# RMS norm statistics with tokens on partitions, in a two-block transformer kernel on one core

## The chip, the cores and the metric

The kernel runs on one core of one Trainium2 chip. The metric is the device time of the core in microseconds, the median of several runs; lower is better. The profile is of one separate execution.

## The reference

One sequence goes through a first block (gated linear attention layer, then an S5 layer, each with attention over a memory of 256 tokens) and a second block (an RWKV and pooling layer with an MLP, then a differential attention layer with an MLP). All of it is float32, width 1024, 512 tokens; the second block puts 16 meta tokens ahead, which makes 528. What the change touches is the norm:

```python
def rms_norm(x, w):
    xf = x.astype(jnp.float32)
    y = xf * lax.rsqrt(jnp.mean(xf * xf, axis=-1, keepdims=True) + EPS)
    return (y * w.astype(jnp.float32)).astype(x.dtype)

mem_n = rms_norm(mem, mem_norm_w)                 # 256 tokens
for i in range(DEPTH):                            # first block
    h = rms_norm(x, norm_w[i])
    ...
    x = x + y @ w_out[i]
x = rms_norm(x, final_norm_w)
for i in range(DEPTH):                            # second block
    hn = rmsnorm(h, g[0]); m = mixer(hn)
    h = h + rmsnorm(m, g[1])
    f = sq_relu_mlp(rmsnorm(h, g[2]))
    h = h + rmsnorm(f, g[3])
```

## The kernel before

All activations lie with features on the 128 partitions and tokens along the free axis: a tensor of width 1024 is eight tiles k of 128 features by 512 or 528 tokens. With 528 tokens a PSUM bank (512 float32 columns) doesn't hold a row of them, so such work goes in two halves of 264 (`HALVES`, line 45). Weights come in units of 128x1024 through a ring of four buffers, loaded by the sync engine. Most matrix products (class `Gemm`, line 101) split both operands into a rounded high part and a low rest and add three products (lines 256, 259, 261). ScalarE makes the high part of each weight unit (`make_high`, line 358), GpSimd the low part (`make_low`, line 349), and TensorE waits for the low part before it begins a unit.

Each engine has its own program. The kernel is a list of stages, and each engine goes through that list in the same order, doing its part of each stage; between engines there are only counting semaphores (`squared`, `summed`, `rooted`, `inverted`, `normed` and others for the norms). The numbers a stage waits for are worked out when the kernel is built, from `b.norms`, a table of how far each semaphore has counted.

A norm is the stage `Rms` (line 462). The squares of the tiles are written by ScalarE. For norms with `added=True` the squares are made while the matrix product ahead of the norm stores its tiles, and VectorE adds them up (`add`, line 521) but for the last, so that TensorE has only two groups of products left (lines 558 and 562). For the others TensorE takes the squares of each k as they come (line 568), ScalarE being at most two squares ahead. These products multiply a 128x128 matrix of ones by the squares, so that every partition of the result has the sum over features, for each token. ScalarE then takes the root of sum / width + eps (line 543), VectorE the reciprocal of the whole 128 by tokens tile (line 580) into `b.inv`, and then scales tile after tile (line 588). Depending on the norm VectorE also adds the result onto x (`onto`, line 585) or subtracts the high part from it (`hi`, `lo`, lines 549 and 593). When the norm feeds a product, ScalarE makes the first high part of its weights directly behind the root (line 546), before the high parts of the tiles.

In the list there are nine such norms and, inside the gated linear attention, four more over 512 features per head. The nine: the memory's (256 tokens) and the first layer's (512 tokens), one behind the other at the start and followed on VectorE by the S5 tables (line 1083) and on TensorE by the memory's key product (line 266 in the profile); the S5 layer's, ahead of the product u; the final norm of the first block; ahead of the second block's first product (528 tokens, not added); behind ev_out and behind the first MLP (528 tokens); behind od_out and behind the last MLP (512 tokens). Behind three of the last four stands a `LateRms` (line 605), a norm whose statistic is worked out while its product already runs on unscaled values; it stays as it is. Its `scalar` starts with the high part of weight unit 1, and it waits for the x tiles that the norm before it finishes. `TokenInverse` (line 685) turns the reciprocals of one late norm into columns with products that move a single column (line 696).

The profile's line numbers are those of the code printed here.

Of the kernel before, what the change touches and what calls it, by code (L numbers as in the profile page):

```python
# [17 lines left out]
ACT = mybir.ActivationFunctionType  # L18
# [5 lines left out]
P = 128  # L24
D = 1024
KD = D // P
# [435 lines left out]
class Rms(Stage):  # L462
# [2 lines left out]


    def __init__(self, b, x, n, ranges, width, eps, w, out, banks, needs, stay=(), view=None, onto=None,
                 hi=None, lo=None, each=None, added=False):
        self.each = each
        self.added = added  # L470
        self.b, self.x, self.n, self.ranges, self.width = b, x, n, ranges, width
        self.eps, self.w, self.out, self.banks, self.needs, self.stay = eps, w, out, banks, needs, stay
        self.view = view or (lambda ap: ap)
        self.onto = onto
        self.at = dict(b.norms)
        self.tokens = sum(w for _, w in ranges)
        b.norms["squared"] += n
        b.norms["summed"] += 1 if added else n
        b.norms["added"] += n - 2 if added else 0
        b.norms["rooted"] += len(ranges)  # L480
        b.norms["inverted"] += 1
        b.norms["ready"] += n
        self.rooted = (b.rooted, b.norms["rooted"])
        self.ready = (b.normed, b.norms["ready"])
        self.tile = lambda k: (b.normed, self.at["ready"] + k + 1)
        if onto:
            self.tile = lambda k: (b.summed_onto, self.at["summed_onto"] + k + 1)
            b.norms["summed_onto"] += n
            self.ready = (b.summed_onto, b.norms["summed_onto"])
        self.feeds = None  # L490
        self.hi, self.lo = hi, lo
        if hi:
            b.norms["parts"] += n
            self.ready = (b.out_lo, b.norms["parts"])
# [34 lines left out]
    def scalar(self, act):  # L529
        b, at = self.b, self.at  # L530
# [8 lines left out]
        act.wait_ge(b.summed, at["summed"] + (1 if self.added else self.n))  # L539
        if at["inverted"]:  # L540
            act.wait_ge(b.inverted, at["inverted"])
        for bank, (t0, tn) in zip(self.banks, self.ranges):
            b.nc.scalar.activation(b.root[:, t0:t0 + tn], b.ps[:, bank, 0:tn], ACT.Sqrt,
                                   bias=b.eps[self.eps], scale=1.0 / self.width).then_inc(b.rooted, 1)
        if self.feeds:
# [5 lines left out]
    def tensor(self, pe):  # L551
        b, at = self.b, self.at
        for s, v in self.stay:
            pe.wait_ge(s, v)
        if self.added:
            pe.wait_ge(b.added, at["added"] + self.n - 2)
            for bank, (t0, tn) in zip(self.banks, self.ranges):
                b.nc.tensor.matmul(b.ps[:, bank, 0:tn], b.ones[:, :], b.sq[:, 0, t0:t0 + tn], start=True, stop=False)
            pe.wait_ge(b.squared, at["squared"] + self.n)
            last = self.slot(self.n - 1)  # L560
            for bank, (t0, tn) in zip(self.banks, self.ranges):
                ins = b.nc.tensor.matmul(b.ps[:, bank, 0:tn], b.ones[:, :], b.sq[:, last, t0:t0 + tn], start=False, stop=True)
            ins.then_inc(b.summed, 1)
            return
        for k in range(self.n):
            pe.wait_ge(b.squared, at["squared"] + k + 1)
            for bank, (t0, tn) in zip(self.banks, self.ranges):
                ins = b.nc.tensor.matmul(b.ps[:, bank, 0:tn], b.ones[:, :], b.sq[:, k % 2, t0:t0 + tn],  # L568
                                         start=(k == 0), stop=(k == self.n - 1))
            ins.then_inc(b.summed, 1)  # L570

    def vector(self, dve):
        b, at = self.b, self.at
        if self.added:
            for k in range(self.rest, self.n - 1):
                self.add(dve, k)
        dve.wait_ge(*self.rooted)
        if at["ready"]:
            dve.wait_ge(b.normed, at["ready"])
        b.nc.vector.reciprocal(b.inv[:, 0:self.tokens], b.root[:, 0:self.tokens]).then_inc(b.inverted, 1)  # L580
        dve.wait_ge(b.inverted, at["inverted"] + 1)
        for k in range(self.n + 2):
            if self.onto and 1 <= k <= self.n:
# [222 lines left out]
class Gla(Stage):  # L806
# [6 lines left out]
    def __init__(self, b, m, z, needs):  # L813
# [22 lines left out]
        for h in range(GLA_HEADS):  # L836
            o = m.o[h]
            last = min(4 * h + 5, self.steps)
            self.rms.append(Rms(b, lambda k, o=o: o[:, k, :], DV // P, FULL, DV, EPS,
                                lambda k: b.col("gla_out_norm_w", k), lambda k, o=o: o[:, k, :], [0],  # L840
                                [(self.saved, 4 * h + 4)], [(self.masked, last), (self.token_keys, last)]))
# [1902 lines left out]
def build(nc, a, out):  # L2744

    with ExitStack() as ctx:
        b = Board(nc, ctx)
# [9 lines left out]
        tables = constants()  # L2757
# [109 lines left out]
        def mix_tile(s):  # L2867
            if s < KD:
# [17 lines left out]
        rms = Rms(b, lambda k: mem[:, k, :], KD, MEMS, D, EPS, lambda k: b.col("mem_norm_w", k),  # L2886
                  lambda k: b.memn[:, k, :], [0], [loads_in], [loads_in])
# [38 lines left out]
        tables = S5Tables(b, t5, a, [rms.ready, (b.summed, 2 * KD)])  # L2926
# [530 lines left out]
```

## Time and profile before

| | us |
|---|---|
| median of 3 runs | 3248.36 |
| lowest, highest run | 3247.49, 3256.5 |
| the profiled execution's own time | 3260.21 |
| its span, first to last instruction | 3257.9 |
| TensorE products busy | 2957.2 (91%) |
| TensorE weight loads busy | 2403.1 (74%) |
| VectorE busy | 1383.3 (42%) |
| GpSimd busy | 1070.2 (33%) |
| ScalarE busy | 970.0 (30%) |

The profile calls the engines PE (products), PEld (weight loads), DVE, ACT, POOL and SP. Products are pipelined, so PE's busy time is not PE at its peak. The chain of waits follows the work that ended last back from the end, step by step. PEclk is the clock granted to TensorE as a share of 2.4 GHz; its mean over the span is 0.959. A float32 product appears as two passes, each with a weight load (LDWEIGHTS) and a MATMUL. Its shape is given as result type, so 128x264 means 264 moving columns.

### The profile page before, as it was taken

Reading aid. Unit: us, or ns where it says so; the run is one execution under the profiler, and the core shown is the slowest. Engines: PE = TensorE matmul, PEld = TensorE weight load, DVE = VectorE, ACT = ScalarE, POOL = GpSimd, SP = SyncE. Lnnn points to the kernel's source line nnn. Section 1 sums busy time; section 2 is a strip of 40 time slices with the busy share of each in tenths; the row PEclk is TensorE's granted clock in tenths of the full one; section 3 lists DMA queues with packets and bytes.
Section 4 is the critical chain, followed back from the end, with each engine's and each line's share of the span. In section 5 each row is a group of like instructions: output and inputs, shape, how many; then the busy total and the mean of one; then the engine's idle time right before and its main releaser. Section 6 shows DMA issues by size and latency. Waiting matters only on the chain.

```text
span 3257.9 us, 45682 instructions
## 1 busy us (share of the span) xinstructions
PE 2957.2 (91%) x18278; PEld 2403.1 (74%) x18278; DVE 1383.3 (42%) x2233; ACT 970.0 (30%) x1551; POOL 1070.2 (33%) x743
## 2 busy tenths in 40 slices
PE   6887899899899899998978887899998989989997
PEld 4666467677788488786767775799996857768886
DVE  5787264510217511202158453470724055374352
ACT  2222254222212246323244332312123115431221
POOL 0332022444324078444422200144443330234442
PEclk9998899999999899999999996999999989999999
DMA  4897011244562279222221000222222200122222
GB/s 141 262 278 247 7 52 44 68 145 152 172 190 95 78 195 245 92 96 78 92 69 59 22 3 20 65 91 89 89 89 79 84 26 1 39 71 97 97 91 78
DMA packets 130704, 324.96 MB, mean 100 GB/s; under 512 B 54096, under 2 KB 54736, under 8 KB 129760
## 3 DMA queue, kind: packets, MB, share of 16 engines
q1 hardware_dynamic: 95904, 221.29, 21.2%
q0 software_dynamic: 30272, 88.88, 9.7%
q10 hardware_dynamic: 4352, 12.25, 1.0%
q8 instruction: 133, 2.18, 0.3%
q14 instruction: 43, 0.35, 0.0%
HBM read 288.38 MB, written 33.95 MB: 99 GB/s over the span
## 4 chain that ended last, share of the span: by engine, by line
PE 71%; DVE 17%; DMA 4%; issue 3%; POOL 2%; ACT 2%; DVEq 0%; ACTq 0%; SPq 0%; POOLq 0%
PE ps L256 17%; PE ps L259 16%; PE ps L261 16%; PE ps L266 3%; DMA d_pb<-arena 3%; PE ps L2473 2%; DVE h L588 1%; PE ps L738 1%; PE ps L568 1%; POOL ring_r L349 1%; PE ps L748 1%; PE ps L2484 1%; DVE inv L580 1%; PE ps L1591 1%; PE ps L1332 1%
## 5 line engine op out<-in xcount | busy, mean ns | idle before, releaser
L349 POOL TENSOR_TENSOR ring_r<-ring,high 128x1024 fp32r<-128x1024 f32 x327 | 819.6, 2506 | 1574.1 <-ACT high L358 1573.9
L256 PE MATMUL ps<-h_hi,high 128*128 128x512 f32 (+1 forms) x2112 | 733.4, 356 | 51.4 <-POOL ring_r L349 18.5
L261 PE MATMUL ps<-h_hi,ring_r 128*128 128x512 f32 (+1 forms) x2112 | 661.1, 348 | 0.0
L358 ACT ACTIVATE high<-ring 128x1024 fp32r<-128x1024 f32 x359 | 379.5, 1057 | 896.3 <-PE ps L256 769.5
L259 PE MATMUL ps<-h_r,high 128*128 128x512 f32 (+1 forms) x1920 | 643.9, 345 | 0.0
L256 PEld LDWEIGHTS ps<-h_hi,high 128*128 128x128 f32 x2112 | 400.7, 190 | 130.3 <-issue 59.3
L261 PEld LDWEIGHTS ps<-h_hi,ring_r 128*128 128x128 f32 x2112 | 370.2, 190 | 53.3
L259 PEld LDWEIGHTS ps<-h_r,high 128*128 128x128 f32 x1920 | 365.7, 190 | 41.8 <-issue 1.4
L259 PE MATMUL ps<-f_r,high 128*128 128x264 f32 (+1 forms) x832 | 261.2, 326 | 0.0
L256 PE MATMUL ps<-f_hi,high 128*128 128x264 f32 (+1 forms) x768 | 236.6, 321 | 0.0
L256 PE MATMUL ps<-z_hi,high 128*128 128x512 f32 x488 | 197.0, 404 | 16.5 <-POOL ring_r L349 10.7
L261 PE MATMUL ps<-f_hi,ring_r 128*128 128x264 f32 (+1 forms) x768 | 205.0, 321 | 0.0
L261 PE MATMUL ps<-z_hi,ring_r 128*128 128x512 f32 x488 | 192.5, 394 | 0.0
L259 PEld LDWEIGHTS ps<-f_r,high 128*128 128x128 f32 x832 | 156.8, 188 | 14.4
L2831 ACT ACTIVATE arena<-ps 128x512 f32<-128x512 f32 (+4 forms) x102 | 58.2, 574 | 331.7 <-PE ps L261 242.4
L256 PEld LDWEIGHTS ps<-f_hi,high 128*128 128x128 f32 x768 | 144.4, 188 | 11.4
L259 PE MATMUL ps<-z_lo,high 128*128 128x512 f32 x360 | 145.3, 404 | 0.0
L261 PEld LDWEIGHTS ps<-f_hi,ring_r 128*128 128x128 f32 x768 | 127.0, 188 | 11.0
L3264 DVE CAST f_hi<-f x64 | 128.9, 2014 | 8.5 <-DVE f L3262 1.2
L256 PEld LDWEIGHTS ps<-z_hi,high 128*128 128x128 f32 x488 | 92.9, 190 | 44.7 <-issue 14.2
L259 PE MATMUL ps<-z_hi,high 128*128 128x512 f32 x280 | 112.2, 401 | 0.0
L261 PEld LDWEIGHTS ps<-z_hi,ring_r 128*128 128x128 f32 x488 | 93.4, 191 | 22.4
(433 smaller groups left out, 4419.7 us busy)
## 6 DMA issues: line engine op xcount, KB each, us to landing
ring<-in_units SPq DMA_DIRECT2D x402, 512.0 KB, 3.3
d_ca<-arena POOLq DMA_DIRECT2D x16, 640.0 KB, 9.5
arena<-d_ca POOLq DMA_DIRECT2D x16, 640.0 KB, 7.2
arena<-d_q POOLq DMA_DIRECT2D x32, 256.0 KB, 8.2
d_pb<-arena POOLq DMA_DIRECT2D x16, 512.0 KB, 11.1
arena<-d_pb POOLq DMA_DIRECT2D x16, 512.0 KB, 4.1
arena<-d_ca POOLq DMA_DIRECT2D x16, 512.0 KB, 5.0
arena<-d_k POOLq DMA_DIRECT2D x128, 64.0 KB, 4.1
```

The lines of the kernel that those rows point to most:

```text
L256: part = mm(acc, hi[:, cols], self.x_hi(k)[:, t0:t0 + tn], start=(k == 0), stop=False)
L259: mm(acc, hi[:, cols], self.x(k)[:, t0:t0 + tn], start=False, stop=False)
L261: ins = mm(acc, w[:, cols], self.x_hi(k)[:, t0:t0 + tn], start=False, stop=(k == self.kt - 1))
L266: ins = mm(acc, w[:, k % 8 * P:(k % 8 + 1) * P], self.x(k)[:, t0:t0 + tn], start=(k == 0), stop=(k == self.kt - 1))
L349: eng.tensor_tensor(b.ring_r[:, slot, :], b.ring[:, slot, :], self.high[:, j % 2, :], ALU.subtract).then_inc(b.unit_lo, 1)
L358: b.nc.scalar.activation(self.high[:, j % 2, :], b.ring[:, u % RING, :], ACT.Copy).then_inc(b.unit_hi, 1)
L568: ins = b.nc.tensor.matmul(b.ps[:, bank, 0:tn], b.ones[:, :], b.sq[:, k % 2, t0:t0 + tn], start=(k == 0), stop=(k == self.n - 1))
L580: b.nc.vector.reciprocal(b.inv[:, 0:self.tokens], b.root[:, 0:self.tokens]).then_inc(b.inverted, 1)
L588: b.nc.vector.scalar_tensor_tensor(out=self.out(k), in0=self.view(self.x(k)), scalar=self.w(k), in1=self.view(b.inv[:, 0:self.tokens]), op ...
L2473: ins = mm(to, m.prob[:, j % 3, c, k0:k0 + kn], m.diag[:, j % 2, c, :], start=(c == 0), stop=(c == 1))
L2831: return nc.scalar.activation(to, ps, ACT.Copy, scale=1.0 if scale is None else scale)
L3264: nc.vector.tensor_copy(hi, t).then_inc(mlp_parts, 1)
```

## The change

`Rms` gets an argument `turned`, true for all but the four norms of the gated linear attention. A turned norm has the squares as stationary operand, 88 tokens at a time (528 = 6 x 88) or 128 (512 = 4 x 128, 256 = 2 x 128), and one column of ones as moving operand: the sum of each token then lies on its own partition, in one column per tile. Root and reciprocal are taken of this block of 88x6 (128x4, 128x2) numbers, both into the tile `b.root`. To have the reciprocals on every partition again, TensorE multiplies: the stationary operand is one column of reciprocals read with a step of zero as 128 columns, the moving one the identity, so each result column is one token's reciprocal on all partitions. ScalarE copies the result from PSUM into `b.inv`. The scalings are unchanged.

```diff
@@ Rms.__init__
-        b.norms["summed"] += 1 if added else n
+        b.norms["summed"] += (1 if added else n) + (1 if turned else 0)
-        b.norms["rooted"] += len(ranges)
+        b.norms["rooted"] += 2 if turned else len(ranges)
+        self.turned = turned
+        self.rows = 88 if self.tokens % P else P
+        self.tiles = [(o, slice(o * self.rows, (o + 1) * self.rows)) for o in range(self.tokens // self.rows)]
@@ Rms.scalar, behind the waits for the sums and the last reciprocal
+        if self.turned:
+            rows, many = self.rows, len(self.tiles)
+            b.nc.scalar.activation(b.root[0:rows, 0:many], b.ps[0:rows, self.banks[0], 0:many], ACT.Sqrt,
+                                   bias=b.eps[self.eps][0:rows], scale=1.0 / self.width).then_inc(b.rooted, 1)
+            act.wait_ge(b.summed, at["summed"] + (1 if self.added else self.n) + 1)
+            first, parts, wide = self.banks[0], len(self.ranges), self.ranges[0][1]
+            b.nc.scalar.activation(b.inv[:, 0:self.tokens].rearrange("p (r t) -> p r t", r=parts),
+                                   b.ps[:, first:first + parts, 0:wide], ACT.Copy).then_inc(b.rooted, 1)
-        for bank, (t0, tn) in zip(self.banks, self.ranges):
+        for bank, (t0, tn) in [] if self.turned else zip(self.banks, self.ranges):
@@ Rms.tensor, each place with products of ones; self.spread(pe) also behind the last of them
+            if self.turned:
+                ins = self.token_sums(pe, k % 2, k == 0, k == self.n - 1)
+    def token_sums(self, pe, slot, start, stop):
+        b = self.b
+        for o, tok in self.tiles:
+            ins = b.nc.tensor.matmul(b.ps[0:self.rows, self.banks[0], o:o + 1], b.sq[:, slot, tok], b.ones[:, 0:1],
+                                     start=start and o == 0, stop=stop and o == len(self.tiles) - 1)
+        return ins
+    def spread(self, pe):
+        if not self.turned:
+            return
+        b, rows = self.b, self.rows
+        pe.wait_ge(b.inverted, self.at["inverted"] + 1)
+        per = len(self.tiles) // len(self.ranges)
+        for o, _ in self.tiles:
+            at = o % per * rows
+            ins = b.nc.tensor.matmul(b.ps[:, self.banks[0] + o // per, at:at + rows],
+                                     b.root[0:rows, 8 + o:9 + o].broadcast_to([rows, P]), b.ident[0:rows, 0:rows],
+                                     start=True, stop=True)
+        ins.then_inc(b.summed, 1)
@@ Rms.vector
-        dve.wait_ge(*self.rooted)
-        b.nc.vector.reciprocal(b.inv[:, 0:self.tokens], b.root[:, 0:self.tokens]).then_inc(b.inverted, 1)
+        if self.turned:
+            rows, many = self.rows, len(self.tiles)
+            dve.wait_ge(b.rooted, at["rooted"] + 1)
+            b.nc.vector.reciprocal(b.root[0:rows, 8:8 + many], b.root[0:rows, 0:many]).then_inc(b.inverted, 1)
+            dve.wait_ge(*self.rooted)
+        else:
+            (as before)
```

## Rows read from the trace of the kernel before

**Rows 1.** The page's chain of waits, whole span: shares by engine, by line
```profile
PE 71%; DVE 17%; DMA 4%; issue 3%; POOL 2%; ACT 2%; DVEq 0%; ACTq 0%; SPq 0%; POOLq 0%
PE ps L256 17%; PE ps L259 16%; PE ps L261 16%; PE ps L266 3%; DMA d_pb<-arena 3%; PE ps L2473 2%; DVE h L588 1%; PE ps L738 1%; PE ps L568 1%; POOL ring_r L349 1%; PE ps L748 1%; PE ps L2484 1%; DVE inv L580 1%; PE ps L1591 1%; PE ps L1332 1%
```
**Rows 2.** Line 580: durations min/median/max in ns, first and last start, forms
```profile
L580 DVE RECIPROCAL inv<-root x13: 1752/3352/3453, 27.9 to 3240.9; 128x512 f32<-128x512 f32 x9, 128x528 f32<-128x528 f32 x3, 128x256 f32<-128x256 f32 x1
```
**Rows 3.** Chain in order of time, from 2072 us: start, length, what
```profile
2073.74 1.13 PE ps L558 x4
...
2075.79 0.86 ACT root L543 x2
...
2076.68 3.46 DVE inv L580
...
2080.16 0.78 DVE h L588
...
2080.97 0.71 DVE x L585
```
**Rows 4.** The same chain, from 3238 us
```profile
3238.02 0.14 issue
3238.16 1.10 PE ps L558 x2
...
3240.15 0.70 ACT root L543
...
3244.25 0.76 DVE h L588
```
**Rows 5.** Instructions of line 696 (as rows 2), then their stretch of the timeline
```profile
L696 PEld LDWEIGHTS ps<-c_ident,inv x10: 93/192/192, 2578.8 to 2579.8; 128*128 128x128 f32 x8, 128*16 128x16 f32 x2
...
2578.94 1.08 PE L696 MATMUL ps<-c_ident,inv 128*128 128x1 f32 x10
```
**Rows 6.** Small operations: count | busy us, mean ns | idle; last a timeline row
```profile
L2596 DVE RECIPROCAL arena<-arena 128x2 f32<-128x2 f32 x32 | 5.1, 160 | 0.3
L2512 ACT ACTIVATE arena<-ps,arena 128x16 f32<-128x16 f32 x16 | 4.3, 268 | 0.0
...
2073.03 0.60 ACT L2831 ACTIVATE h<-ps 128x528 f32<-128x528 f32 x1
```
**Rows 7.** Timeline of the first two norms: start, length, engine, line [idle before]
```profile
27.28 0.47 ACT L543 ACTIVATE root<-ps,c_eps 128x256 f32<-128x256 f32 x1
...
28.32 7.53 PE L568 MATMUL ps<-sq,c_ones 128*128 128x512 f32 x16 [1.60 <-ACT sq L538]
...
36.67 13.62 PE L266 MATMUL ps<-memn,ring 128*128 128x256 f32 x62 [0.82 <-issue]
...
54.52 15.77 PE L266 MATMUL ps<-memn,ring 128*128 128x256 f32 x64 [3.79 <-ACT arena L2831]
```
**Rows 8.** Timeline ahead of the product u
```profile
811.58 1.28 ACT L543 ACT_TABLE_LOAD   x1
...
814.59 2.33 POOL L349 TENSOR_TENSOR ring_r<-ring,high 128x1024 fp32r<-128x1024 f32 x1 [1.08 <-ACT high L358]
816.98 3.26 DVE L588 SCALAR_TENSOR_TENSOR h<-x,cols,inv 128x512 f32<-128x512 f32 x3
```
**Rows 9.** Timeline and chain of the second block's first norm
```profile
1647.80 10.32 PE L568 MATMUL ps<-sq,c_ones 128*128 128x264 f32 x32 [5.63 <-ACT sq L538]
...
1662.52 2.12 DVE h L588 x3
...
1671.72 1.05 ACT high L358
```
**Rows 10.** Stretches of 1 us: length, PE PEld DVE ACT POOL busy (x), PEclk, DMA
```profile
1642.00:1643.00 1.00, 0.17 (x1) 0.00 (x0) 0.07 (x1) 0.69 (x1) 1.00 (x3) 1.00 0.77 316
...
1646.00:1647.00 1.00, 0.00 (x0) 0.00 (x0) 0.96 (x3) 0.00 (x0) 0.00 (x0) 0.62 0.54 197
...
1652.00:1653.00 1.00, 1.00 (x4) 0.80 (x3) 0.00 (x0) 0.42 (x1) 0.00 (x0) 0.50 0.00 0
```

More of the change, by code:

```diff
@@ L467, in __init__ @@
     def __init__(self, b, x, n, ranges, width, eps, w, out, banks, needs, stay=(), view=None, onto=None,
-                 hi=None, lo=None, each=None, added=False):
+                 hi=None, lo=None, each=None, added=False, turned=True):
         self.each = each
@@ L556, in tensor @@
             pe.wait_ge(b.added, at["added"] + self.n - 2)
-            for bank, (t0, tn) in zip(self.banks, self.ranges):
+            if self.turned:
+                self.token_sums(pe, 0, True, False)
+            for bank, (t0, tn) in [] if self.turned else zip(self.banks, self.ranges):
                 b.nc.tensor.matmul(b.ps[:, bank, 0:tn], b.ones[:, :], b.sq[:, 0, t0:t0 + tn], start=True, stop=False)
@@ L560, in tensor @@
             last = self.slot(self.n - 1)
-            for bank, (t0, tn) in zip(self.banks, self.ranges):
+            if self.turned:
+                ins = self.token_sums(pe, last, False, True)
+            for bank, (t0, tn) in [] if self.turned else zip(self.banks, self.ranges):
                 ins = b.nc.tensor.matmul(b.ps[:, bank, 0:tn], b.ones[:, :], b.sq[:, last, t0:t0 + tn], start=False, stop=True)
             ins.then_inc(b.summed, 1)
+            self.spread(pe)
             return
@@ L566, in tensor @@
             pe.wait_ge(b.squared, at["squared"] + k + 1)
-            for bank, (t0, tn) in zip(self.banks, self.ranges):
+            if self.turned:
+                ins = self.token_sums(pe, k % 2, k == 0, k == self.n - 1)
+            for bank, (t0, tn) in [] if self.turned else zip(self.banks, self.ranges):
                 ins = b.nc.tensor.matmul(b.ps[:, bank, 0:tn], b.ones[:, :], b.sq[:, k % 2, t0:t0 + tn],
@@ L570, in tensor @@
             ins.then_inc(b.summed, 1)
+        self.spread(pe)
+    def token_sums(self, pe, slot, start, stop):
[16 more added lines that the diff above has]
+        ins.then_inc(b.summed, 1)
     def vector(self, dve):
@@ L576, in vector @@
                 self.add(dve, k)
-        dve.wait_ge(*self.rooted)
         if at["ready"]:
             dve.wait_ge(b.normed, at["ready"])
-        b.nc.vector.reciprocal(b.inv[:, 0:self.tokens], b.root[:, 0:self.tokens]).then_inc(b.inverted, 1)
+        if self.turned:
+            rows, many = self.rows, len(self.tiles)
[3 more added lines that the diff above has]
+        else:
+            dve.wait_ge(*self.rooted)
+            b.nc.vector.reciprocal(b.inv[:, 0:self.tokens], b.root[:, 0:self.tokens]).then_inc(b.inverted, 1)
         dve.wait_ge(b.inverted, at["inverted"] + 1)
@@ L840, in __init__ @@
                                 lambda k: b.col("gla_out_norm_w", k), lambda k, o=o: o[:, k, :], [0],
-                                [(self.saved, 4 * h + 4)], [(self.masked, last), (self.token_keys, last)]))
+                                [(self.saved, 4 * h + 4)], [(self.masked, last), (self.token_keys, last)], turned=False))
         self.done = (self.multiplied, z.body_outs * z.iters)
@@ L2925, in build @@
         t5.par = view(14336, 13, 192)
-        tables = S5Tables(b, t5, a, [rms.ready, (b.summed, 2 * KD)])
+        tables = S5Tables(b, t5, a, [rms.ready, (b.summed, 2 * KD + 2)])
         stages.append(tables)
```

## The prediction

> **What bounds the kernel now.** I read the chain of waits first. It stands on TensorE for 71% of the span and on VectorE for 17%, and the norms' scalings and reciprocals (lines 588 and 580) have 1% each in its rounded shares [rows 1]. The matmuls take most of the time, so what matters is where TensorE stands still. The lines view gives the reciprocal thirteen times at about 3.35 us [rows 2]. Nine of these belong to the norms that the change turns; four are the gated linear attention's, which keep the old way. The chain in order of time shows a norm behind a matmul stage: products with ones, root, reciprocal, first scaling, first sum, each released by the one before, with TensorE quiet from the sums to the next stage's first product [rows 3, 4]. These are stretches in which time saved reaches the end.
>
> **The price of the new pieces.** The nearest thing to the new products is line 696, five float32 products with one moving column. Each is two passes of weight load and product; ten passes start in 1.08 us, of which two load 16 columns, so a 128-column pass costs about 0.12 us and the last result needs 0.14 us more [rows 5]. The other pieces: a reciprocal of 128x2 takes 0.16 us, an activation of 128x16 from PSUM 0.27 us, a 128x528 copy out of PSUM 0.60 us [rows 6]. I put the small root at 0.25, the small reciprocal at 0.16, the copy at 0.60 (0.40 for 256 tokens, between the last two), and 0.04 per handover, as between root and reciprocal in [rows 3].
>
> **From root to first scaling.** Before, with 528 tokens: 2075.79 to 2080.16, 4.37 us [rows 3]. After, with six tiles of 88: 0.25 root + 0.04 + 0.16 reciprocal + 0.04 + spreading + 0.04 + 0.60 copy + 0.04. The spreading is six products, twelve passes, each loading 128 columns (one column of reciprocals broadcast): 12 x 0.12 + 0.14 = 1.58. Sum 2.75, saved 1.62. With 512 tokens before: 3240.15 to 3244.25, 4.10 us [rows 4]; after, with four tiles, eight passes: 0.96 + 0.14 = 1.10, sum 2.27, saved 1.83.
>
> **The sums.** With 512 tokens, four products of 512 columns (ones by the sum so far and by the last square, each in two passes) run from 3238.16 to the root at 3240.15, 1.99 us [rows 4]; sixteen new passes cost 16 x 0.12 + 0.14 = 2.06, a loss of 0.1. With 528 tokens, eight passes of 264 columns take 2073.74 to 2075.79, 2.05 us [rows 3]; the new twenty-four load 88 columns each. In [rows 5] a 16-column load takes 93 ns where a 128-column one takes 192, and interpolated that is 155 ns for 88, so I take 0.10 per pass: 2.4 + 0.14 = 2.54, a loss of 0.5. Bounds for a pass: 0.075 (the loads alone, scaled) to 0.12, so the sums gain 0.1 or lose 1.0.
>
> The Trainium skill, "TensorE: Matmul & The Clock Gate", section "Part 2: What happens when you issue a matmul", says the weight load's time goes with the columns loaded and not with the rows. By it an 88-column pass would be 88/128 of 0.12, an estimate of 0.083 us, and the sums of 528 tokens would take 2.1 us and lose 0.1 instead of 0.5; by the row of this trace the load shortens less than in proportion. The same rule gives the spreading nothing for its 88 rows, as I have counted.
>
> **Norm by norm.**
> - The memory's norm and the first norm (27 to 40 us). The squares of the second now stand behind the first's copy on ScalarE. Before, they stood behind the first root, which ends at 27.75 [rows 7]. Now: root from 27.28, 0.25 + 0.04 + 0.16 + 0.04 + two tiles spread (four passes, 0.62) + 0.04 + copy 0.40 = 28.83, so 1.1 us late. The eight sums were sixteen passes in 7.53 us, 0.94 each k; sixty-four new passes at 0.12 are 7.7, a loss of 0.2 to 0.5. Then the chain from the root saves 1.83. Net saved 0.3. Also, the memory's key product starts on the second norm's copy instead of its root, 1.4 late and 2.23 instead of 0.70 behind the root's start, so at 39.6 instead of 36.67; this is covered, since TensorE later waits 3.79 us for ScalarE to empty its banks, until 54.52 [rows 7]. Without the cover it would cost 2.9.
> - Norm ahead of the product u (813 us). The root follows a table load that ends at 812.86 behind other ScalarE work, so nothing in the sums matters; from the root on 1.83 saved. The high part of the next weights (line 358, 1.05 us) and its POOL half (2.33 us) used to hide under the reciprocal [rows 8]. They now start behind the copy: counted from the root's start, 2.23 + 1.05 + 0.05 + 2.33 = 5.7 us, while the first lower half h_r, behind three scalings, is there at 2.27 + 3 x 1.09 + 0.7 = 6.2. Still hidden, by 0.5.
> - Final norm of the first block (1642 us), 512 tokens: 1.83 - 0.1 = 1.7.
> - First norm of the second block (1648 to 1671 us), not added up on VectorE: eight steps of sums. Before, 10.32 us for thirty-two passes [rows 9], the first half of it at a granted clock of 0.50, 1.2 GHz [rows 10]. New: ninety-six passes. At full clock 9.6 + 0.14 = 9.7, a gain of 0.6; if the first 3.7 us stay at half clock, 11.4, a loss of 1.1. Before, the clock fell 4 us after TensorE's last product, with TensorE quiet in between; now the spreading stands in the middle of that quiet. I take 0. From the root 1.62 saved. The weights' high and low parts now end 2.7 + 1.05 + 2.33 = 6.1 us after the root's start, and the first lower half of h at 2.75 + 2.12 + 0.7 = 5.6, so TensorE begins 0.5 later than VectorE would allow; but the first tile goes by VectorE's pace, and the second starts only on the high part made at 1671.72 [rows 9], behind all of ScalarE's work on h, which moves with VectorE. So 1.6.
> - Norms behind ev_out and the first MLP (2076, 2469 us), 528 tokens: 1.62 - 0.5 = 1.1 each. The free high part of unit 1 behind the copy (1.06 us) stays under the first scaling and sum (1.5 us, [rows 3]).
> - Norms behind od_out and the last MLP (2866, 3241 us), 512 tokens: 1.7 each. The last one ends in the output's DMAs, which follow tile by tile.
>
> Sum: 0.3 + 1.8 + 1.7 + 1.6 + 1.1 + 1.1 + 1.7 + 1.7 = 11.0 us. VectorE also loses some 27 us of busy time, worth nothing beyond this. The profiled execution took 3260.21 us (span 3257.9); minus 11.0 it is 3249.2. The runs' median is 3248.36, 11.85 under the profiled one, so the forecast for the median is 3237.4 us.
>
> **Bounds.** The sum hangs on the pass, since there are 64 + 96 + 2 x 24 + 3 x 16 of them in sums on the path and 5 x 8 + 3 x 12 in spreadings. Below: 0.10 in the spreadings and 0.075 in the sums of 88 columns take 1.5 and 3.6 off, 16 us saved. Above: 0.13 for every pass adds 0.8 in the spreadings, 2.9 at 1648, 0.7 at 2076 and at 2469, 0.6 at 28 and 0.5 in the sums of 512 tokens, 5 us saved. Own range of the forecast: 3232 to 3243.
>
> **Rivals.**
> 1. *Half clock in the new products (slower).* The two long runs of sums, at 28 and 1646 us, become runs of one-column products, and the granted clock falls to 0.50 in them. For it: after TensorE's quiet the clock is at 0.50 for 6.8 us [rows 10], and in no row does a run of one-column products last longer than 1.1 us. Against: the weight loads keep TensorE occupied throughout, and line 696 ran at 1.00. Price: at half clock a pass doubles. Sixty-four at 0.24 are 15.4 instead of 7.5 us, ninety-six at 0.20 are 19.2 instead of 10.3: 16.8 us more. If the spreadings are caught as well, five cost 8 x 0.12 and three 12 x 0.12 more, 9 us in all. It decides from 11 us, that is when both runs are caught. Outcome: -11 + 17 to -11 + 26, +6 to +15, middle 3259 us. The Trainium skill, "TensorE: Matmul & The Clock Gate", section "Part 1: The HAM clock gate (the "warmup" mystery)", says that the clock is throttled by default and that activity releases it; by it this rival depends on whether such products count, which no row here settles.
> 2. *A narrow pass costs more than in line 696 (no change).* At 0.15 us a pass the spreadings lose 2.3, the sums at 1648 4.8, those at 2076 and 2469 2.4, those at 28 1.9 and those of 512 tokens 1.4: 12.8 us, which leaves +2, 3250 us. For it: nothing here loads a broadcast column as weights, or strings so many loads together, and VectorE's handover to TensorE took 0.14 us [rows 4] where I count 0.04. Against: the ten passes of [rows 5], back to back behind other work.
> 3. *The first savings are given back.* Those at 28 and 813 us feed stages in which DMAs also bound work; then only the second block's and the final norm's 8.9 us stay: 3239.5 us. Against: the chain at both places runs through VectorE. This lies in the forecast's own range and I count it there.
>
> **How the numbers follow.** What a measurement of this kernel can tell from no change is 0.3%, 9.7 us. Forecast (with rival 3) 60%, centre 3237.4, of which seven in ten pass 9.7 us. Rival 1 22%, two thirds of it beyond +9.7. Rival 2 18%, all within. Faster 0.60 x 0.72 = 0.43; slower 0.14; same 0.43. The range takes the forecast's own and rival 2, and the lower half of rival 1: 3231 to 3258.
>
> **What would show it.** The small reciprocal on 88 and 128 partitions at about 0.16 us nine times; copies of 0.6 us into inv; root to first scaling 2.75 and 2.27 us; the sums at 1648 near 10 us and at 28 near 8 us with the granted clock beside them. Wrong it would be if a pass costs over 0.15 us, if the clock is at 0.50 in either run of sums, or if the quiet behind a norm has not become shorter where root to scaling has.

## The result, and the profile after

The changed kernel takes 3268.82 us (median of 4 runs, 3262.95 to 3273.97) against 3250.56 us of the kernel before in the same session (4 runs, 3247.49 to 3256.5). The ratio is 1.0044, 95% interval 1.0023 to 1.0065: slower by 0.4%. The profiled execution has a span of 3268.1 us at a mean granted clock of 0.956; before it was 3257.9 us at 0.959. The forecast was 3237.4 us.

First the new pieces, each line's instructions with the shortest, median and longest duration in ns; they answer to [rows 2, 5, 6].

```profile
L623 DVE RECIPROCAL root<-root x9: 165/178/188, 28.1 to 3251.1; 128x4 f32<-128x4 f32 x5, 88x6 f32<-88x6 f32 x3, 128x2 f32<-128x2 f32 x1
...
L547 ACT ACTIVATE root<-ps,c_eps x9: 262/263/265, 27.7 to 3250.7; 128x4 f32<-128x4 f32 x5, 88x6 f32<-88x6 f32 x3, 128x2 f32<-128x2 f32 x1
...
L551 ACT ACTIVATE inv<-ps x9: 384/597/612, 29.6 to 3253.4; 128x512 f32<-128x512 f32 x5, 128x528 f32<-128x528 f32 x3, 128x256 f32<-128x256 f32 x1
```

Root, reciprocal and copy cost about what was forecast (0.25, 0.16, 0.60). What comes out wrong stands in three other places. The timeline of the first two norms (start, length, engine, line), to be read beside [rows 7]:

```profile
27.73 0.26 ACT L547 ACTIVATE root<-ps,c_eps 128x2 f32<-128x2 f32 x1
...
30.53 13.81 PE L595 MATMUL ps<-c_ones,sq 128*128 128x1 f32 x64 [0.99 <-ACT sq L541]
...
44.38 0.26 ACT L547 ACTIVATE root<-ps,c_eps 128x4 f32<-128x4 f32 x1 [2.79 <-PE ps L595]
...
47.78 4.61 PE L266 MATMUL ps<-memn,ring 128*128 128x256 f32 x10 [0.73 <-issue]
```

The sixty-four one-column passes take 13.81 us, 0.216 each, where 16 wide ones took 7.53. TensorE is never idle in these 13.81 us. The second norm's first scaling comes at 47.72 us instead of 39.99, and the memory's key product at 47.78 instead of 36.67.

What the clock was in this run has to be read from durations, because the column PEclk can't be relied on this early: in every profile it reads 1.00 from the start to its first fall, also where TensorE works at half pace. These are the clock's row (columns as below), the run's weight loads, those of the sixteen wide passes before, and the loads of the same form in the changed kernel's sums at 1644 us, where the durations agree with the 1.00 of the column (ns: shortest, median, longest):

```profile
30.53:44.34 13.81, 13.81 (x64) 13.72 (x64) 2.72 (x7) 4.24 (x7) 0.00 (x0) 1.00 0.01 1
L595 PEld LDWEIGHTS ps<-c_ones,sq x64: 287/333/333, 30.5 to 43.9; 128*128 128x128 f32 x64
L568 PEld LDWEIGHTS ps<-sq,c_ones x16: 186/189/190, 28.3 to 34.8; 128*128 128x128 f32 x16
L595 PEld LDWEIGHTS ps<-c_ones,sq x16: 186/192/192, 1643.6 to 1645.3; 128*128 128x128 f32 x16
```

A load of 128 columns that takes 192 ns at 1.00 takes 333 here, and 333 is also what it takes in the spreading at 1665 us, where PEclk reads 0.50. So the run went at half clock, by its durations and not by the column. In the kernel before, the loads take 333 ns only in the memory norm's first sums, from 20.4 to some 24 us, and then 190.

The second block's first norm, beside [rows 9], and then the granted clock around it (length, PE, PEld, DVE, ACT, POOL busy with counts, PEclk, DMA share, GB/s), beside [rows 10]:

```profile
1650.16 14.24 PE L595 MATMUL ps<-c_ones,sq 128*88 128x1 f32 x96 [2.15 <-ACT sq L541]
...
1665.05 2.86 PE L608 MATMUL ps<-c_ident,root 88*128 88x88 f32 x12 [0.64 <-DVE root L623]
...
1668.59 4.21 DVE L635 SCALAR_TENSOR_TENSOR h<-x,cols,inv 128x528 f32<-128x528 f32 x3 [3.60 <-ACT inv L551]
...
1669.59 2.65 POOL L349 TENSOR_TENSOR ring_r<-ring,high 128x1024 fp32r<-128x1024 f32 x1 [22.91 <-ACT high L358]
```

```profile
1645.00:1647.00 2.00, 1.37 (x10) 1.28 (x10) 0.18 (x1) 0.26 (x1) 1.68 (x4) 0.86 0.87 297
1647.00:1650.00 3.00, 1.01 (x5) 0.72 (x4) 1.32 (x2) 1.13 (x2) 0.00 (x0) 0.50 0.93 271
1650.00:1664.00 14.00, 13.84 (x95) 13.84 (x95) 4.07 (x7) 4.61 (x8) 0.00 (x0) 0.50 0.01 2
1664.00:1668.00 4.00, 3.27 (x15) 2.95 (x15) 0.19 (x1) 0.32 (x2) 0.00 (x0) 0.50 0.00 0
1668.00:1676.00 8.00, 2.43 (x11) 2.46 (x12) 7.41 (x9) 4.53 (x7) 2.65 (x1) 0.50 0.10 25
```

For 14 us TensorE is busy 13.84 us with products and with loads, and the clock stays at 0.50, 1.2 GHz. Before, it was back at full within the wide sums. These are the neighbouring stretches of the kernel before:

```profile
1647.00:1650.00 3.00, 2.20 (x5) 1.80 (x6) 3.00 (x6) 1.29 (x2) 0.00 (x0) 0.50 0.00 0
1650.00:1658.00 8.00, 8.00 (x28) 5.69 (x27) 1.70 (x3) 3.86 (x6) 0.00 (x0) 0.81 0.00 0
1658.00:1662.00 4.00, 0.12 (x1) 0.00 (x0) 2.96 (x1) 1.80 (x3) 1.97 (x1) 1.00 0.00 0
```

The three scalings in the norm's rows above take 4.21 us instead of the 2.12 of [rows 9], and GpSimd works beside them. The norm behind ev_out, timeline, beside [rows 3], has the same thing:

```profile
2082.32 2.76 PE L595 MATMUL ps<-c_ones,sq 128*88 128x1 f32 x24 [1.25 <-issue]
2085.12 0.26 ACT L547 ACTIVATE root<-ps,c_eps 88x6 f32<-88x6 f32 x1 [2.90 <-PE ps L595]
2085.48 0.19 DVE L623 RECIPROCAL root<-root 88x6 f32<-88x6 f32 x1 [10.14 <-ACT root L547]
2085.72 2.86 PE L608 MATMUL ps<-c_ident,root 88*128 88x88 f32 x12 [0.64 <-DVE root L623]
2088.62 0.61 ACT L551 ACTIVATE inv<-ps 128x528 f32<-128x528 f32 x1 [3.24 <-PE ps L608]
2089.12 1.05 ACT L358 ACTIVATE high<-ring 128x1024 fp32r<-128x1024 f32 x1
2089.26 0.77 DVE L635 SCALAR_TENSOR_TENSOR h<-h,cols,inv 128x528 f32<-128x528 f32 x1 [3.60 <-ACT inv L551]
2090.07 0.71 DVE L632 TENSOR_TENSOR x<-x,h 128x528 f32<-128x528 f32 x1
2090.25 2.73 POOL L349 TENSOR_TENSOR ring_r<-ring,high 128x1024 fp32r<-128x1024 f32 x1 [105.59 <-ACT high L358]
2090.69 2.85 DVE L635 SCALAR_TENSOR_TENSOR h<-h,cols,inv 128x528 f32<-128x528 f32 x1
```

Here the clock fell inside the sums, from 1.00 in the microsecond from 2082 to 0.50 in that from 2084, and they take 2.76 us; the experiments below show 2.01 for the same passes at 1.00. Two things more: the spreading takes 2.86 us, 0.24 a pass, so that root to first scaling is 4.14 us against 4.37 in [rows 3]; and the second scaling takes 2.85 us where one takes 0.77, because it meets GpSimd's low part. In the kernel before, the high part was made behind the root and the low part ran beside the reciprocal [rows 8]. Its company didn't lengthen the reciprocal: over 512 tokens it takes 3.35 us at 813.59 beside GpSimd, and 3.35 at 36.61 with GpSimd idle.

How far each place lies behind the kernel before, in us: first scaling of the second norm 7.7; start of the attention 8.6; first reciprocal of the gated linear attention 4.1; small reciprocal ahead of u 3.1; at 1645 us 3.0; at 1664 us 5.8; at 2085 us 8.8; at 2106 us 11.2; at 2480 us 11.0; at 2875 us 8.6; the end 10.2. In these two profiles the attention gives back 4.5 of the first loss, but over all profiles it doesn't. The first reciprocal of the gated linear attention starts at 475.0 to 484.1 us in the eight profiles whose first two norms are as before (482.1 in the kernel before), and at 485.6 to 493.1 in the four that have them turned with no product added, 9.3 later on average. The scatter of 8 to 9 us within each group is as large as the effects looked for: in 320 to 480 us the mean granted clock of the profiled executions lies between 0.86 and 0.94, with no order by kernel, and the kernel before alone ranged from 3242.3 to 3265.7 us over 33 runs. I rest the parts below on ratios and on the durations of instructions.

### The profile page after: what moved, and what is told of

Read it like the earlier page. It is cut to its first block, busy times and chain, and to the rows that moved or that the text cites. A ratio compares the mean times of both kernels' runs of the same rounds, so it can differ in the third digit from the quotient of the medians.

```text
span 3268.1 us, 46273 instructions
## 1 busy us (share of the span) xinstructions
PE 2983.3 (91%) x18566; PEld 2445.6 (75%) x18566; DVE 1365.9 (42%) x2233; ACT 971.6 (30%) x1557; POOL 1064.0 (33%) x743
## 4 chain that ended last, share of the span: by engine, by line
PE 71%; DVE 17%; DMA 4%; issue 3%; POOL 2%; ACT 2%; DVEq 0%; ACTq 0%; SPq 0%; POOLq 0%
PE ps L256 16%; PE ps L259 16%; PE ps L261 16%; PE ps L266 3%; DMA d_pb<-arena 2%; DVE h L635 2%; PE ps L2520 1%; PE ps L595 1%; PE ps L785 1%; PE ps L795 1%; PE ps L2531 1%; PE ps L1638 1%; PE ps L1379 1%; POOL ring_r L349 1%; PE ps L1469 1%
```

## The experiments

Each ratio is against the kernel before in the same session, with its 95% interval; the runs of one kernel are 6 to 12, those of the kernel before 25 to 33. They are told by question. "Turned" is a norm with the new statistics, "added" one whose squares VectorE sums first (six of the nine).

**Which norms lose?** Turned only where added, then only where not.

```diff
+        self.turned = turned = turned and added          # e2_added
+        self.turned = turned = turned and not added      # e4_long
```

> The changed kernel with only the six norms turned whose squares VectorE adds up (two groups of sums each); the memory's, the first layer's and the second block's first norm are as before the change. Theory A: the long runs of one-column products are gone, so are their 6.3 and 3.9 us and the spreadings at half clock there; 8 to 12 us less than the changed kernel, 3257 to 3261, still above the kernel before because of the POOL collisions at 813, 2090 and 2879 us. Rival (the loss is spread evenly over all nine norms): a third of it goes, near 3262.

> Only the three norms that VectorE doesn't add up are turned (the memory's and the first at 20 to 48 us, the second block's first at 1645 us); the six others are as before. Theory (the change's parts add up, and the long runs of sums at half clock are what makes it slower): the run at 28 us takes 13.8 instead of 7.5 us and that at 1645 us 14.2 instead of 10.3, the scaling behind the latter 4.2 instead of 2.1 us; 7 to 8 us lost at the first and 2 to 4 at the second, ratio 1.003 to 1.005, which times the 0.9997 of the six others alone gives the 1.0044 of the whole change. Rival (the loss at 28 us is given back behind it, where transfers and the half clock of the attention set the pace): ratio 1.000 to 1.001, and the whole change's 1.0044 has no owner.

Measured: 3251.1 us, ratio 0.9997 (0.9981 to 1.0012), for the six; 3264.31 us, 1.0035 (1.0018 to 1.0052), for the three. Their product is 1.0032, inside the interval of the whole. So the three norms that VectorE doesn't add up carry most of the loss, some 11 us, and the six bring no measurable gain. In the profile of the three, the runs of sums take what they took in the whole change: 13.81 us at 30.63 and 14.24 us at 1648.87.

**Is it the clock, and do wider products free it?** Once 64 columns of ones move in each sum instead of one, once a wide product of the old kind stands ahead of each k's sums.

```diff
-            ins = b.nc.tensor.matmul(b.ps[0:self.rows, self.banks[0], o:o + 1], b.sq[:, slot, tok], b.ones[:, 0:1],
+            ins = b.nc.tensor.matmul(b.ps[0:self.rows, self.banks[0], 64 * o:64 * o + 64], b.sq[:, slot, tok], b.ones[:, 0:64],
```
```diff
+                b.nc.tensor.matmul(b.ps[:, 6, 0:self.ranges[0][1]], b.ones[:, :],
+                                   b.sq[:, k % 2, 0:self.ranges[0][1]], start=True, stop=True)
                 ins = self.token_sums(pe, k % 2, k == 0, k == self.n - 1)
```

> The changed kernel with one edit: the sums move 64 columns of ones instead of one (the results stand 64 times side by side, the root reads every 64th column). Weight loads, their count and their order are the same. Theory A (the clock is at 0.50 in the two long runs of sums because of what is moved): the granted clock is at 1.00 again in most of both runs, the sums at 28 us take about 8 us instead of 13.8 and those at 1650 about 10 instead of 14.2, some 10 to 12 us less than the changed kernel, near 3258. Rival B (a narrow pass costs about 0.2 us by its weight load, whatever is moved): both runs as long as before or longer, time unchanged near 3268.

> The changed kernel, with one product of the old kind (ones by 256, 512 or 264 columns of squares, two passes) ahead of each k's one-column sums in the three norms that are not added up on VectorE; it adds work of no use. Theory (wide moving operands raise the granted clock, weight loads do not): the clock goes to 1.00 in both runs; one-column passes take 0.12 us at 128 columns and 0.083 us at 88; the run at 28 us is then 8 x (0.94 + 0.96) = 15.2 us and that at 1645 us 8 x (0.5 + 1.0) = 12 us, 2 less than the 14.2 us of the change in spite of the added work. Rival (the clock stays down for another reason, such as the one-column products pulling it down whatever stands between): passes stay at 0.21 and 0.147 us, the wide ones double, and the runs take 27 and 21 us.

Measured: 64 columns, 3263.0 us, 1.0025 (1.0009 to 1.0041); with the wide products 3292.49 us, 1.0115 (1.0093 to 1.0137). The row of the timeline of the first at the second block's first norm, then its clock (columns as above):

```profile
1643.33 14.34 PE L595 MATMUL ps<-c_ones,sq 128*88 128x64 f32 x96 [2.15 <-ACT sq L541]
```
```profile
1643.00:1658.00 15.00, 14.34 (x96) 14.16 (x96) 4.24 (x7) 5.04 (x9) 0.00 (x0) 0.50 0.01 2
```

The same two of the second:

```profile
1663.69 1.23 PE L584 MATMUL ps<-sq,c_ones 128*128 128x264 f32 x2
1664.71 1.83 PE L597 MATMUL ps<-c_ones,sq 128*88 128x1 f32 x12
```
```profile
1670.00:1680.00 10.00, 10.00 (x56) 9.05 (x54) 0.00 (x0) 1.93 (x3) 0.00 (x0) 0.50 0.01 2
```

Both of my forms of the idea fell. In the second block's first norm the clock was 0.50 throughout in both, with TensorE busy 10.00 of 10 us in the second; in the first layer's norm the median load of 128 columns took 333 ns in both, as in the change. A pass with 64 moving columns costs what one with a single column does (0.149 against 0.148 us), so the moved columns don't set the price; the pass follows its load. With the wide products each step at 1660 us takes 2.70 us and each at 38 us 3.41, so the runs of eight steps take 21.6 and 27.3 us, the rival's 21 and 27. That the passes are slow because of the clock shows the other way round, in stretches at 1.00: sixteen passes of 128 columns take 1.92 us and twenty-four of 88 take 2.01, against 0.216 and 0.148 a pass here. What would have brought the clock back within these runs stays open. What is shown is that neither form brought it back, and that in the kernel before the clock came back to 1.00 while the wide sums ran. It is no chance of two profiles: the sums at 1633 to 1650 us take 14.24 to 14.34 us in the four that have them narrow alone, and 9.74 to 10.56 in the eight that have them wide.

**Is it GpSimd beside the scalings?** In the changed kernel, the high part of the next weights right behind the small root instead of behind the copy; and in the kernel before, the high part held until the long reciprocal is done, with nothing turned.

```diff
@@ e3_high, Rms.scalar, behind the small root
+            if self.feeds:
+                self.feeds.make_high(act, 0, 0)
+            if self.early:
+                self.early.make_high(act, 1, 0, free=True)
             act.wait_ge(b.summed, at["summed"] + (1 if self.added else self.n) + 1)
@@ e5_collide, Rms.scalar of the kernel before, behind the roots
+        if self.feeds or self.onto:
+            act.wait_ge(b.inverted, at["inverted"] + 1)
```

> The changed kernel with one move: ScalarE makes the first high part of the next weights right behind the small root instead of behind the copy into inv, so that GpSimd's low part (2.35 us) runs mostly under reciprocal and spreading and no more beside the first scalings. Theory C (a VectorE scaling beside GpSimd's subtraction takes 2.85 us instead of 0.76): the long scalings at 819, 1669, 2090 and 2879 us are gone or shortened, 1.5 to 2 us each, 5 to 8 us less than the changed kernel, near 3262. Rival D (the scaling is long for another reason, such as the half clock or the copy just ahead): the 2.8 us stay and so does the time, near 3268.

> The kernel before the change, with one wait added: in the norms that feed a product or add onto x, ScalarE makes the next weights' first high part only when the reciprocal is done, so GpSimd's low part falls on the first scalings instead of the reciprocal. Nothing of the change is in it. Theory C: one scaling in each of four or five norms takes 2.8 us instead of 0.76, 6 to 10 us more than the kernel before, near 3258. Rival D: scalings as before, at most 1 to 2 us more for the later weights, near 3252.

Measured: 3261.02 us, 1.0017 (1.0004 to 1.0031), for the first; 3265.57 us, 1.0032 (1.0018 to 1.0046), for the second. The timeline of the first, at the norm behind ev_out, and of the second, at the same norm:

```profile
2080.30 1.04 ACT L358 ACTIVATE high<-ring 128x1024 fp32r<-128x1024 f32 x1
2080.74 2.87 PE L612 MATMUL ps<-c_ident,root 88*128 88x88 f32 x12 [0.64 <-DVE root L627]
2081.42 2.34 POOL L349 TENSOR_TENSOR ring_r<-ring,high 128x1024 fp32r<-128x1024 f32 x1 [102.00 <-ACT high L358]
...
2084.29 0.77 DVE L639 SCALAR_TENSOR_TENSOR h<-h,cols,inv 128x528 f32<-128x528 f32 x1 [3.60 <-ACT inv L555]
2085.72 0.76 DVE L639 SCALAR_TENSOR_TENSOR h<-h,cols,inv 128x528 f32<-128x528 f32 x1
```

```profile
2081.44 3.45 DVE L582 RECIPROCAL inv<-root 128x528 f32<-128x528 f32 x1 [9.92 <-ACT root L543]
2084.93 1.06 ACT L358 ACTIVATE high<-ring 128x1024 fp32r<-128x1024 f32 x1 [3.52 <-DVE inv L582]
...
2086.07 2.59 POOL L349 TENSOR_TENSOR ring_r<-ring,high 128x1024 fp32r<-128x1024 f32 x1 [105.73 <-ACT high L358]
2086.36 2.85 DVE L590 SCALAR_TENSOR_TENSOR h<-h,cols,inv 128x528 f32<-128x528 f32 x1
```

With the high part early the scalings are back at 0.77 and 0.76 us (and at 3.34 for three at 827 us, 2.12 for three at 1667, 0.83 at 2873); with it late, the kernel before gets the same 2.85 us. It has them in the four places of the changed kernel (5.35 us for three at 810, 4.21 for three at 1663, 2.85 at 2086, 2.83 at 2878), 2.1 us more each, 8.4 in all, and is slower by 10.4 us (5.9 to 15 by its interval). Moving the high part in the changed kernel takes off 0.27%, 8.8 us, from another session's ratio, but the two intervals overlap. The run with 64 columns, which has all four long scalings and the same long sums, came out at 1.0025 in the same session, only 0.08% above. So the collision is shown from both sides in the durations; what it costs in time is shown from one side, by the second experiment.

The Trainium skill, "SBUF — State Buffer", section "Who interferes with whom", says that a VectorE instruction with two inputs in SBUF contends with a GpSimd instruction that reads SBUF, that one with at most one input outside the 2-port modes doesn't, that the shared ports are an exclusive lock, and that the order of issue decides who waits. The traces agree: the scaling that starts at 2090.69, behind GpSimd's start at 2090.25, ends 0.56 us after GpSimd's row has ended at 2092.98, and the reciprocals, with one input, ran beside the same operation at their usual 3.35 us.

**What is left of the idea without both?** Only the added norms turned, with the high part early.

```diff
+        self.turned = turned = turned and added          # and the edit of e3_high
```

> Only the six norms whose squares VectorE adds up are turned, and in them ScalarE makes the high part of the next weights right behind the small root, ahead of the wait for the spreading. Theory (the change's loss is the long runs of sums at half clock plus GpSimd's low part falling on VectorE's first scalings): both terms are gone, the first scalings take 0.76 us again in all places, root to first scaling stays 3.1 to 3.3 us (512 tokens) and about 4.15 us (528), that is 0.8 to 1.0 us less than before four times and 0.2 us twice. Together some 4 us less than the kernel before, ratio 0.998 to 0.999, and 5 to 8 us less than with these norms turned alone. Rival (the high part in front delays nothing but the scalings were not on the path either): the time equals that of the added norms alone, ratio 1.000.

Measured: 3249.79 us, ratio 0.9985 (0.9969 to 1.0001). The theory's value, but no change lies within the interval. The first scalings take 0.75 to 0.84 us, root to first scaling 4.15 us at 2068, since twelve spreading passes still take 2.86 us. At 2856 us even the sums are caught: sixteen passes take 2.86 us instead of 1.92.

**Is the spreading slow by its broadcast column, or by the clock?** The same kernel, with products of no use while TensorE would be idle, in the four norms behind a matmul stage; and the same products in the kernel before, as a control.

```diff
+    def warm(self, pe, widths):
+        for wide in widths if self.onto else []:
+            b.nc.tensor.matmul(b.ps[:, 5, 0:wide], b.ones[:, :], b.ones[:, 0:1].broadcast_to([P, wide]), start=True, stop=True)
+        if self.onto:
+            self.warm(pe, [512, 256])
         for s, v in self.stay:
             pe.wait_ge(s, v)
@@ behind the sums
             ins.then_inc(b.summed, 1)
+            self.warm(pe, [256])                         # e11_before_warm: [512] * 6, no spread
             self.spread(pe)
+            self.warm(pe, [512] * 3)
```

> The kernel with only the added norms turned and the high part in front, and idle TensorE given products of no use in the four norms behind a matmul stage of the blocks (2070, 2460, 2860, 3230 us): 512 and 256 columns ahead of the wait for the added squares, 256 between sums and spreading, three of 512 behind the spreading, into a bank that nothing reads. Theory (the spreading is slow because TensorE was quiet and the clock fell): spreadings go from 2.08 and 2.86 us to about 1.1 and 1.5 us, the next stage's first four products of 264 columns from 2.10 us to about 1.2; 1.0 to 1.4 us saved four times and up to 1 more three times, 5 to 8 us below the kernel without them, ratio to before about 0.996. Rival (loading a broadcast column as weights costs 0.24 us by itself): spreadings stay at 2.08 and 2.86 us, and the time stays or grows by up to 2 us for products that end late.

> The kernel before, nothing turned, with products of no use in the same four norms: 512 and 256 columns ahead of the wait for the added squares, six of 512 columns between the sums and the next stage. It tells how much of what such products bring is theirs and not that of the turned statistics. Theory: sums stay at 2.0 us, the next stage's first products run at full clock, 0 to 2 us saved three times, ratio 0.998 to 1.000. Rival: TensorE's first products waited for ScalarE's and VectorE's parts anyway, so nothing is saved, ratio 1.000.

Measured: 3250.25 us, 0.9984 (0.9970 to 0.9998), and 3255.29 us, 0.9995 (0.9983 to 1.0008) for the control. Timeline of the first, then its clock:

```profile
2070.79 0.19 DVE L638 RECIPROCAL root<-root 88x6 f32<-88x6 f32 x1 [9.39 <-ACT root L547]
2071.03 1.57 PE L623 MATMUL ps<-c_ident,root 88*128 88x88 f32 x12
2071.71 2.34 POOL L349 TENSOR_TENSOR ring_r<-ring,high 128x1024 fp32r<-128x1024 f32 x1 [102.23 <-ACT high L358]
...
2073.28 1.33 DVE L650 SCALAR_TENSOR_TENSOR h<-h,cols,inv 128x528 f32<-128x528 f32 x1 [2.31 <-ACT inv L555]
```
```profile
2068.00:2078.00 10.00, 8.65 (x52) 5.64 (x52) 4.80 (x7) 4.02 (x7) 2.34 (x1) 1.00 0.00 0
```

Twelve passes take 1.57 us where they took 2.86, and their weight loads a median of 190 ns (333 in the change), as any load of 128 columns at 1.00 does: the broadcast column costs nothing of its own, the clock does. But the products held the clock only in part (the spreadings at 2463 and 3232 us took 2.65 and 2.05), and where they did, the scaling came early enough to meet GpSimd's low part again: 1.33 us here, 1.59 at 2860. At two of the four places part of the gain turned into the other wait, and the time is that of the kernel without these products (0.9985). The control shows that such products alone bring nothing measurable.

**Both together.** The high part ahead of the root's wait for the sums, where ScalarE is idle; and then one more product of no use between the two halves of the sums.

```diff
         act.wait_ge(b.summed, at["summed"] + (1 if self.added else self.n))     # the two calls of make_high now stand ahead of this
@@ e14_earlier_mid, Rms.tensor
                 self.token_sums(pe, 0, True, False)
+                self.warm(pe, [256])
```

> The kernel with only the added norms turned and products of no use around sums and spreading, in which the high part of the next weights is made ahead of the root's wait for the sums, not behind the root. With the quicker spreading GpSimd's low part (2.34 us) reached into the first scaling again (1.59 instead of 0.76 us at 2860 us). Theory (that is where the quicker spreading was given back): the low part ends before the first scaling, which takes 0.76 us in all four places, and the time is 1 to 4 us below the kernel with the high part behind the root, ratio about 0.997. Rival (ScalarE gets the weights' part late and the root with it): the root starts up to 1 us later than the sums allow, and the time is the same or higher.

> The kernel just above (high part ahead of the sums), and one more product of no use, 256 columns, between the two halves of the one-column sums. Theory (a stretch of one-column products counts for the clock as idle, as in the 24 passes after which it fell at 2460 us; a wide one between them holds it): the clock stays at 1.00 until the first scaling in all four places, spreadings take 1.1 and 1.57 us for 2.05 and 2.65, 0.43 us lost for 1.0 gained three times; 1 to 2 us below the kernel without it. Rival (a single product between doesn't matter): the clock falls at the same places, sums 0.43 us longer four times, up to 2 us slower.

Measured: 3246.25 us, 0.9980 (0.9967 to 0.9994), the lowest ratio of all; with the product between, 3253.01 us, 0.9997 (0.9981 to 1.0012). Timeline of the first at the last norm:

```profile
3221.74 0.26 ACT L552 ACTIVATE root<-ps,c_eps 128x4 f32<-128x4 f32 x1 [2.04 <-PE ps L611]
3222.11 0.18 DVE L639 RECIPROCAL root<-root 128x4 f32<-128x4 f32 x1 [2.46 <-ACT root L552]
3222.34 1.16 PE L624 MATMUL ps<-c_ident,root 128*128 128x128 f32 x8
...
3223.53 0.60 ACT L556 ACTIVATE inv<-ps 128x512 f32<-128x512 f32 x1 [1.53 <-PE ps L624]
3224.16 0.75 DVE L651 SCALAR_TENSOR_TENSOR h<-h,cols,inv 128x512 f32<-128x512 f32 x1 [1.88 <-ACT inv L556]
```

Root to first scaling is 2.42 us here and at 2849, 2.86 at 2064, 3.32 at 2455; the first scaling takes 0.75 to 0.77 us in all four. The product between the halves did not keep the clock at 2459 us (twelve passes in 2.86 us), and it makes the sums longer by 0.43 to 0.48 us each; that one fell. The intervals overlap with each other and with that of the added norms with the high part early (0.9985). So only the first's gain over the kernel before is established, not its lead over any of the others.

## Why the prediction was wrong

The sign was wrong: 11.0 us of gain were forecast, and 14.3 of loss measured by the ratio. Three terms make the difference: two were priced at the wrong clock, and one stood nowhere in the sum.

- **The sums, 10.2 us.** The step that failed is "sixty-four new passes at 0.12 are 7.7" at 28 us, and "I take 0" for the run at 1648. They took 13.8 and 14.2 us instead of 7.5 and 10.3. This is rival 1, which I gave 22%. My argument against it, that the weight loads keep TensorE occupied, was true and did not matter: the engine was occupied and the clock stayed at 0.50 (at 28 us by the doubled durations, at 1650 by PEclk too). The clock did not fall in these two runs, as rival 1 has it: it was low when they began and did not come back. The row at 1.00 from which I took the price, [rows 5], was 1.1 us long, and tells nothing of a run of 14 us. Rival 1's price for the two runs, 16.8 us, was too high: they cost 10.2. Its 0.24 and 0.20 a pass are 0.216 and 0.148. For the second, the cause is the price at full clock: an 88-column pass is not 0.10 but 2.01 us for twenty-four, 0.084. The Trainium skill's rule that the load goes with its columns ("TensorE: Matmul & The Clock Gate", "Part 2: What happens when you issue a matmul") gave 0.083, the traces agree, and my interpolation from a 16-column load was the worse estimate.
- **The spreadings, some 9 us.** The second: "root to first scaling 2.75 and 2.27 us" measured 4.14 three times and 3.1 to 3.3 five times. The working was right at full clock, where the experiments show 2.86 and 2.42. The products stand behind the wait for root and reciprocal, and the clock was low already or fell in the sums or in that wait. Rival 1 has this term too ("9 us in all"), and there it is right.
- **The weights' low part, 8.4 us.** "Still hidden, by 0.5" at 813, and "stays under the first scaling and sum" at 2076. I asked whether GpSimd ends in time for TensorE, and not whether VectorE works beside it at its usual pace. It doesn't: 2.1 us at four places. Neither forecast nor rivals had this; it is the mechanism that was missing. [Rows 8] had the pair hidden under a reciprocal, and the change took away that reciprocal.
- **The memory's key product.** That its start was "covered, since TensorE later waits 3.79 us" held for as much as that wait could cover: the product started 11.1 us late and not 2.9, ran without the wait, and the value product behind it (line 289 before) started 7.7 late, at 78.46 instead of 70.81. That is as late as the norm itself; the attention started 8.6 late.
- **Right:** the small root, the small reciprocal, the copy, and the sums of 512 tokens (1.95 or 1.96 to the root's start, for 2.06). That the quiet behind a norm is on the path is borne out in part: with the high part early and products of no use around the spreading, the six norms give 0.2%, 6.5 us (2 to 10.7), of which the forecast had 9.1 without either.

By the terms: 11.0 forecast, less 10.2, 9 and 8.4, is 16.6 us slower (0.2 to 0.5 of the 10.2 stood in the forecast already); the ratio says 14.3 (7 to 21), and the two profiled executions differ by 10.2. Rival 1's two terms as measured make 8 us of loss and not 14: without the collision it would not have come to what was measured.

## What to carry to other kernels

Before you swap wide products for many narrow ones, look for a run of narrow ones as long as yours and read the granted clock in it; a busy TensorE is no sign of a fast one. When you remove a long operation, list what ran beside it and see what that runs beside now: GpSimd's low part beside VectorE's two-input scalings cost 2.1 us a time, beside a reciprocal nothing. Compare the granted clock's column with the duration of a known instruction before you believe it. And when a stage gets shorter, check again whether the work that it used to cover still ends before the next step.

## What the runs showed of the hardware that I had not expected

- Ninety-six one-column passes with their loads (TensorE busy 13.84 us of a stretch of 14) did not bring the granted clock from 0.50 to 1.00; neither did 64 moving columns, nor two passes of 264 columns ahead of every twelve narrow ones (10.00 of 10 us busy). The Trainium skill, "TensorE: Matmul & The Clock Gate", section "Part 1: The HAM clock gate (the "warmup" mystery)", has the clock throttled until activity releases it; by these rows a TensorE that is busy in the profile need not be released.
- A column read with a step of zero as 128 columns of weights loads like any other: 190 ns a load and 1.57 us for twelve passes at full clock, 333 ns and 2.86 us at half.
- PEclk reads 1.00 from the start of a profile to its first fall, whatever the pace: in the changed kernel the loads of 128 columns take 333 ns from 20.7 to 44 us under a 1.00, and 192 at 1644 us under the same 1.00.
- A weight load of 88 columns with its narrow product takes 0.084 us and one of 128 columns 0.12, in proportion (24 in 2.01 us, 16 in 1.92, at 1.00).
